# A two-block transformer on one core: the order of work at five seams between stages

## The reference, cut to what matters

```python
mod = cs @ ada_w[l] + ada_b[l]
sh1, sc1, g1, sh2, sc2, g2 = jnp.split(mod, 6, axis=-1)
h = rms_norm(x, norm_mix_g[l]) * (1.0 + sc1[:, None]) + sh1[:, None]
x = x + g1[:, None] * hybrid_mixer(h, w_in[l], w_out[l], ...)
h = rms_norm(x, norm_ffn_g[l]) * (1.0 + sc2[:, None]) + sh2[:, None]
f = swiglu(h, ...) if l % 2 == 0 else moe_ffn(h, ...)
x = x + g2[:, None] * f
...
x = rms_norm(x, final_norm_g)                       # end of the first model
x = x + 0.5 * swiglu_2(rmsnorm(x, ffn1_norm[l]), ffn1_w_gu[l], ffn1_w_down[l])
```

## Time and profile before

| | |
|---|---|
| median of 3 runs | 2380.55 us (2379.64 to 2385.55) |
| profiled execution | 2394.42 us, of which span 2393.1 us, mean granted TensorE clock 0.974 |
| TensorE matmul | busy 2298.8 us, 96% of the span, 10628 instructions |
| VectorE | busy 1705.5 us, 71% |
| ScalarE | busy 1416.7 us, 59% |
| DMA | 571.55 MB, mean 239 GB/s |

### The profile page before, as it was taken

How to read it: one execution, slowest core, us unless ns; L and a number is a source line. 1 busy time by engine, 2 the same in 40 slices (tenths; PEclk the granted TensorE clock), 3 DMA queues, 4 the chain that set the end, 5 groups by cost and what they waited for, 6 DMA issues and landing times.

```text
span 2393.1 us, 34697 instructions
## 1 busy us (share of the span) xinstructions
PE 2298.8 (96%) x10628; PEld 1884.6 (79%) x10628; DVE 1705.5 (71%) x2223; ACT 1416.7 (59%) x2071; POOL 42.2 (2%) x69
## 2 busy tenths in 40 slices
PE   6998999998999999999999989999999999889999
PEld 5776887777888888888887778877888888767887
DVE  4776877766889999998999955577555555744554
ACT  4645444555787777778777754465544544565443
POOL 1000111000000000000000000000000000000000
PEclk8999999999999999999999999999999999979999
DMA  8855887754999999999999945553565555412651
GB/s 300 278 174 181 282 301 267 249 158 109 347 360 356 352 366 353 358 358 354 367 349 357 349 152 185 191 167 117 183 193 177 184 184 176 151 50 62 211 191 55
DMA packets 411218, 571.55 MB, mean 239 GB/s; under 512 B 28111, under 2 KB 324481, under 8 KB 410978
## 3 DMA queue, kind: packets, MB, share of 16 engines
q1 hardware_dynamic: 401200, 543.13, 67.9%
q0 software_dynamic: 6960, 23.79, 3.3%
q10 hardware_dynamic: 2946, 3.22, 0.4%
HBM read 568.99 MB, written 1.05 MB: 238 GB/s over the span
## 4 chain that ended last, share of the span: by engine, by line
PE 85%; DVE 7%; ACT 5%; issue 2%; SPq 1%; DMA 0%; ACTq 0%; DVEq 0%
PE bank L348 76%; DVE lo L327 2%; ACT hi L325 1%; PE bank L543 1%; PE bank L2660 1%; ACT xn L102 1%; SPq L274 1%; PE bank L810 1%; PE bank L2787 1%; ACT aT_hi L102 1%; PE bank L1857 0%; PE bank L2729 0%; DMA raw<-ada_w 0%; DVE small L102 0%; PE bank L1819 0%
## 5 line engine op out<-in xcount | busy, mean ns | idle before, releaser
L327 DVE TENSOR_TENSOR lo<-raw,hi 128x1024 fp32r<-128x1024 f32 x997 | 1177.6, 1221 | 192.1 <-ACT hi L325 178.1
L325 ACT ACTIVATE hi<-raw 128x1024 fp32r<-128x1024 f32 x997 | 1004.4, 1054 | 108.4 <-PE bank L348 99.3
L348 PE MATMUL bank<-hi,aT_hi 128*128 128x512 f32 (+1 forms) x2016 | 814.8, 404 | 23.7 <-DVE aT_lo L102 10.6
L348 PE MATMUL bank<-hi,aT_lo 128*128 128x512 f32 (+1 forms) x2016 | 791.7, 393 | 0.0
L348 PE MATMUL bank<-lo,aT_hi 128*128 128x512 f32 (+1 forms) x2016 | 790.9, 392 | 0.0
L348 PEld LDWEIGHTS bank<-hi,aT_hi 128*128 128x128 f32 x2016 | 383.9, 190 | 106.9 <-issue 17.6
L348 PEld LDWEIGHTS bank<-hi,aT_lo 128*128 128x128 f32 x2016 | 383.1, 190 | 81.8
L348 PEld LDWEIGHTS bank<-lo,aT_hi 128*128 128x128 f32 x2016 | 384.6, 191 | 74.6 <-issue 1.7
L348 PE MATMUL bank<-hi,hidT_hi 128*128 128x512 f32 x792 | 310.1, 392 | 0.9 <-DVE hidT_lo L2668 0.9
L348 PE MATMUL bank<-hi,hidT_lo 128*128 128x512 f32 x792 | 308.4, 389 | 0.0
L348 PE MATMUL bank<-lo,hidT_hi 128*128 128x512 f32 x792 | 308.3, 389 | 0.0
(11 more groups left out here) (330 smaller groups left out, 1609.3 us busy)
## 6 DMA issues: line engine op xcount, KB each, us to landing
raw<-moe_w_gate SPq DMA_DIRECT2D x352, 256.0 KB
raw<-moe_w_up SPq DMA_DIRECT2D x352, 256.0 KB
raw<-moe_w_down SPq DMA_DIRECT2D x176, 512.0 KB
raw<-ffn_w_gu SPq DMA_DIRECT2D x352, 256.0 KB
raw<-ffn_w_down SPq DMA_DIRECT2D x110, 512.0 KB
raw<-ada_w SPq DMA_DIRECT2D x56, 512.0 KB
raw<-w_in SPq DMA_DIRECT2D x56, 512.0 KB
ada_slot<-ada_w POOLq DMA_DIRECT2D x40, 512.0 KB, 6.4
```

The lines of the kernel that those rows point to most:

```text
L325: act.activation(hi[u % SPL][:, :], raw[r % RAW][:, :], ACTF.Copy).then_inc(hi_done, 1)
L327: dve.tensor_tensor(lo[u % SPL][:, :], raw[r % RAW][:, :], hi[u % SPL][:, :].bitcast(F32), ALU.subtract).then_inc(lo_done, 1)
L348: ins = pe.matmul(bank, left[a], right[b], start=first and n == 0, stop=last and n == 2)
```

## The change

It moves work at five seams.

1. `FFN_SLABS` has (0, 11) ahead of (1, 9), so slab (0, 11) ends one step sooner. `at_end` keeps the look-ahead alone. `second_bias` and `second_conditioning` move into the last two steps; there the row of (0, 11) is copied by ScalarE to `mod_rows` and both gate halves are added in one instruction. Of slab (1, 9) the second half, its column sums, four columns of `mod_cols` and the second gain are done by `last_ada_columns` in slot 5 of layer 1's mixer, on bank 5.
2. `modulated_first` calls `run_late(1)` and `run_late()` sooner, between the subtractions.
3. The second tile's squares are summed in one instruction of 1024 (`rstd_whole`), not two halves.
4. In `route_tokens` the second tile's low part (`split_lo(1)`) stands behind the one-hot matrices and the count, and the weights stand in front of the pair. `first_pair` starts with six products that need no second low part; TensorE loads the count between the second and the third bank.
5. In `normed_final` the squares of the first tile's `x` are summed ahead of the second tile's copies, the other three sums behind them.

```diff
-FFN_SLABS = [(0, 10)] + [(1, n) for n in (0, 1, 2, 3, 6, 7, 8, 9)] + [(0, 11)]
+FFN_SLABS = [(0, 10)] + [(1, n) for n in (0, 1, 2, 3, 6, 7, 8)] + [(0, 11), (1, 9)]
...
         def at_end():
-            begin(STEPS - 1, 0, 1)
-            end(STEPS - 1)
             look_ahead(UNITS_D)
...
         h = hi_pair(0, 2, a)
+        run_late(1)
+        done += lo_pair(0, 2, h)
         split_to(st["use"] + 3)
         a = full_pair(0, full_act, 0, turned[2], 4, gain, bias, marks)
-        done += lo_pair(0, 2, h)
         h = hi_pair(0, 4, a)
-        run_late(1)
+        done += lo_pair(0, 4, h)
+        run_late()
         split_to(st["use"] + 4)
-        run_late()
...
+    def rstd_whole(t):
+
+        ss, v, r = tiny(1), tiny(1), tiny(1)
+        a = ACT.run([x_mark[t]], act.activation, xn[:, t, :], x[:, t, :], ACTF.Square, accum_out=ss)
+        a = ACT.run([a], act.activation, v, ss, ACTF.Sqrt, bias=eps_col[:, :], scale=1.0 / D)
+        return r, DVE.run([a], dve.reciprocal, r, v)
...
+    def last_ada_columns():
+
+        n = STEPS - 2
+        ada_sums(n, 0, 1)
+        PE.need(*bank_mark[5])
+        pe.wait_ge(ada_steps, 8 * n + 8)
+        for j in range(4):
+            ins = pe.matmul(psum[5][:, j:j + 1], ada_sum[n % 2][:, j * P:(j + 1) * P], ones_sq[:, 0:1], start=True, stop=True)
+        m = PE.did(ins)
+        m = DVE.run([m], dve.tensor_tensor, mod_cols[:, 28:32], psum[5][:, 0:4], bias_cols[:, 28:32], ALU.add)
+        bank_mark[5] = (m,)
+        mod_marks[:] = [modulated_gain(1, 1, range(8), m)]
...
+            if n == 5 and layer:
+                last_ada_columns()
...
             one_hots()
             busy = count_most(full)
             e, ready = ratio()
-            PE.need(busy)
-            pe.reg_load(most[mybir.EngineType.PE], busiest_i[0:1, 0:1])
-            first_pair()
+            first_hi[:] = [parts[1]]
+            split_lo(1)
+            route["weights"] = weights(eq4, w4, out, e, ready)
+            first_pair(lambda: (PE.need(busy), pe.reg_load(most[mybir.EngineType.PE], busiest_i[0:1, 0:1])))
             split_to(st["use"] + 6)
-            route["weights"] = weights(eq4, w4, out, e, ready)
...
         run_late()
+        sq = square(0, x, pp, [x_mark[0], (moe_y, 4)])
         split_to(st["use"] + 4)
...
-            gained(0)
+            g0 = gained(0)
             done = plain_tile(1, groups, gain)
-            a = gained(1)
+            g1 = gained(1)
+            a = square(0, xg, ss, [g0, sq])
+            b = square(1, x, pp, [x_mark[1]])
+            a = square(1, xg, ss, [g1, b])
```

More of the change, by code:

```diff
@@ L1039, in ada_out @@
         acc = ada_sum[n % 2]
-        if n in (0, STEPS - 2):
+        if n in (0, STEPS - 3):
             pe.matmul(psum[3][:, :], ones_sq[:, :], acc[:, :], start=True, stop=True).then_inc(ada_added, 1)
+            part = slice(0, SLAB) if n == 0 else slice(SLAB, D)
+            dst, src = mod_rows[:, part], psum[3][:, :]
         else:
@@ L1182, in accs_ripe, with second_bias, second_conditioning @@
         return max(0, (st["acc"] - 2) // 4)
[L1184 to L1199, removed]
+    def second_bias():
+        PE.need(bias_in[0])
+        pe.wait_ge(ada_rows, STEPS - 4)
+        pe.transpose(psum[3][:, 32:64], bias_pieces[:, :], ident[0:32, 0:32])
+        ada_out(STEPS - 4)
+        bias_mark[:] = [ACT.run([], act.activation, bias_cols[:, :], psum[3][:, 32:64], ACTF.Copy)]
+    def second_conditioning():
+        dve.wait_ge(ada_rows, STEPS - 2)
+        m = DVE.run(bias_mark, dve.tensor_tensor, mod_cols[:, 0:28], ada_cols[:, 0:28], bias_cols[:, 0:28], ALU.add)
+        DVE.need(gates_in[0])
+        gates_mark[:] = [DVE.did(dve.tensor_tensor(gates[:, 1, :], gates[:, 1, :], mod_rows[:, 0:D], ALU.add))]
+        bank_mark[3] = (m,)
+        mod_marks[:] = [modulated_gain(1, 0, range(8), m)]
     def store_tile(t):
@@ L2259, in route_tokens @@
         r, r_mark, xT_marks, logits, parts = {}, {}, {}, {}, {}
+        first_hi = []
         top, idx = tiny(NT * 8), tiny(NT * 8)
@@ L2353, in one_hots, with first_pair @@
                     route["hot"] = one_hot(DVE, z, t, 2 * z + t)
-        def first_pair():
+        def first_pair(load_count):
             hot = route["hot"]
@@ L2360, in first_pair, with term @@
             mark = {}
[L2361 to L2367, removed]
+            banks = (6, 7, 4, 5)
+            def term(i, kk, n):
+                k, (t, part) = 2 * i + kk, ((0, 0), (0, 1), (1, 0), (1, 1))[n]
+                return pe.matmul(psum[banks[i]][:, kk * S:(kk + 1) * S], xn_split[part][:, t, k * P:(k + 1) * P],
+                                 onehot[:, t, :, :].rearrange("p z s -> p (z s)"), start=n == 0, stop=n == 3)
+            PE.need(hot, parts[0], *first_hi)
+            for i in range(2):
+                PE.need(*bank_mark[banks[i]])
+                for n in range(3):
+                    term(i, 0, n)
+            PE.need(parts[1])
+            for i in range(4):
+                PE.need(*bank_mark[banks[i]])
+                for kk, n in [(0, 3)] if i < 2 else [(0, n) for n in range(4)]:
+                    term(i, kk, n)
+                for n in range(4):
+                    ins = term(i, 1, n)
                 mark[i] = PE.did(ins)
+                if i == 1:
+                    load_count()
             out, hi_mark, lo_mark = {}, {}, {}
@@ L2896, in end @@
         def end(n, i=0):
-            if n == STEPS - 1:
-                second_conditioning(n)
+            if n == STEPS - 3:
+                second_bias()
+            elif n == STEPS - 2:
+                PE.need(*bias_mark)
+                ada_out(n - 1)
+                second_conditioning()
             elif n > 0:
```

19 lines of the change are left out of this document (8 added, 11 removed).

## The result

| | before | changed |
|---|---|---|
| median, 20 runs each | 2386.45 us (2377.74 to 2391.41) | 2379.41 us (2373.73 to 2387.49) |
| ratio | | 0.9977, 95% interval 0.9967 to 0.9988 |
| profiled execution | 2394.42 us, span 2393.1 | 2380.89 us, span 2379.6 |
| mean granted clock, profiled | 0.974 | 0.980 |

The change made the kernel faster by 5.5 us as the ratio has it (2.9 to 7.9), 7.0 us between the medians. 6.1 us was forecast and lies inside; the likeliest verdict given, no change, does not hold, since the interval excludes 1.

What follows compares the result with a forecast made beforehand. TensorE was taken to bound the kernel, with 85% of the chain of waits, so seams count by what it loses there. 1.3 + 4.2 - 9.1 + 2.0 + 7.7 = 6.1 us off 2380.55 gave 2374.4 us, range 2367.5 to 2380.5.

Steps and rivals of the forecast that it cites:

- Term 3: Slot 5 of the mixer: TensorE waits for VectorE's four sums, then columns and slow matmuls follow; cost 9.1 us.
- Rival A: Slot 5 of the mixer: VectorE is not behind, TensorE waits about 2 us; time 2368.2 us; chance 0.12.
- rival C: Mixer slots 8 to 11: VectorE's debt comes back to TensorE, slower than before, 2381.9 us; chance 0.08.
- Terms 1 and 2: Layer 0's feed-forward part: additions come sooner, gaining 1.3 us at its start and 4.2 us at its end.
- Term 4: Routing: VectorE reaches the branch sooner and its wait there stays 4.34 us; gain 2.0 us, bounds 1.0 and 2.5.
- Term 5: Behind the experts: `r_keep` 4.65 us sooner, TensorE's 4.07 us gap becomes 1.2, clock stays up; gain 7.7 us.
- Rival B: Behind `normed_final`: the clock falls there too, so the gain is 4.65 us; time 2377.5 us; chance 0.15.

Runs made afterwards that it cites:

- early_sums: The changed kernel with the second half of the last slab summed right behind the mixer's first slab, not in slot 5; 2371.9 us, ratio 0.9945.
- p1_slabs: The kernel before with only the slab order, second conditioning in the last steps and last slab's columns in slot 5; 2393.78 us, ratio 1.0031.
- p4_routing: The kernel before with only the second low part behind the one-hot matrices and the weights ahead of the pair; 2382.77 us, ratio 0.9984.
- p5_final: The kernel before with only the sums of squares in `normed_final` moved behind the copies; 2378.78 us, ratio 0.9969.
- weights_last: The changed kernel with the seven instructions of the weights back right ahead of the branch; 2380.06 us, ratio 0.9966.
- p23_start: The kernel before with only the second tile's additions between the subtractions and its squares summed in one instruction; 2383.53 us, ratio 0.9975.

## Why the prediction was right or wrong

- **Term 3 (9.1 us at slot 5)** was right: wait 5.55 us for 5.56, columns 1.84 for 1.84, the stretch 9.6 us longer. early_sums shows the cause: the sums' place in VectorE's queue. Rival A falls (TensorE waited 5.55 us, not 2), and C too: from 445 to 531 us the changed kernel's TensorE has no gap of 0.9 us or more.
- **Terms 1 and 2 (1.3 and 4.2)** were right: 8.65 to 7.33 us for the first, a gap of 3.07 us for the forecast 3.1 in the second. Between the two turns p1_slabs takes 197.36 us, p4_routing 201.40 and p5_final 201.38: 4.0 us for term 2. The other 1.1 of the -5.19 are fewer matmuls at the lower level behind the first turn (3 or 4 in place of 8), and p4_routing and p5_final have them too, with no change there.
- **Term 4 (2.0)** was too small: 3.46 us. The failed step is "I take the gap as what VectorE needs to load its register and branch", as a constant of 4.34 us. It became 3.06 with two long low parts right in front of the branch. The end of VectorE's work ahead of the branch came 2.18 us sooner, as forecast (2.05), but not by the forecast's halves of 1.05 and 1.0: in weights_last, where only the low part has moved, it already came 2.03 us sooner, and moving the weights too gave 0.15. That sum was right by luck.
- **Term 5 (7.7)** was too large. `r_keep` came 4.7 us sooner (forecast 4.65), the gap was 1.51 us for 1.2, so TensorE went on 4.4 us sooner. The failed step is "a gap of 1.2 us is of the size that left the clock at 1.00, so the 3.05 us come too": the clock fell behind the short gap in five of the six profiles that have it unfilled, for about half as long, so only 1.3 us came in the changed kernel's. Rival B was half right.
- **The sum**: 1.3 + 4.0 - 9.6 + 3.5 + 5.7 = 4.9 us by the changed kernel's trace, 5.8 at equal clock, 5.5 by the ratio, 6.1 forecast. The two wrong sizes cancel (1.5 too little, 2.0 too much), and that is luck. The profiled executions lie 13.5 us apart; the other 8.5 us are no gain of a seam: 0.3 us ahead of the feed-forward part, 1.1 of clock behind its second turn, 2.6 of clock behind the first expert's wait, and 4.5 in the last stretch.
- **The numbers** failed at "A measurement of this kernel can tell about 0.3%": with 20 runs a side it tells 0.11%, and a gain of 0.23% is no longer "the same". The level, a median of three, was 5.9 us off: the runs' granted clock moves the kernel by more than the change does. And the range, 2367.5 to 2380.5, is said to hold most of rival C, whose own time, 2381.9, lies outside it.

## What to carry to other kernels

Put the work of a side chain so early into its engine's queue that its consumer comes well behind it: the same four sums cost 8.7 us in slot 5 and nothing 7 us earlier, counted from the mixer's first turn. Ahead of a branch, try a long instruction last, with the small chained ones further up; in all profiles here the wait was shorter so. Filling a wait to keep the clock up can pay only where no other engine's chain sets the next wait. And compare runs of about the same granted clock before you believe a difference of a few us.

## What the runs showed of the hardware that I had not expected

- Behind gaps of about the same length the clock falls in one execution and not in another. Ahead of the first expert it fell behind 2.40 us (p4_routing) and not behind 3.56 (p23_start); behind `normed_final` a 1.50 us gap left it up in early_sums alone.
- The mean granted clock of an execution lies between 0.974 and 0.985 for one kernel; the medians of its slowest and fastest group above lie 10.6 us apart.
- VectorE's wait behind one branch is 1.74 to 4.87 us in versions of the same program, by what stands in front of it, while 1.8 to 2.1 us lie between an instruction packet's start and its restart each time. ScalarE's longest idle time around the same branch of the changed kernel is 1.12 us. It ends 1.84 us behind another such packet, which starts while the second of ScalarE's two high parts ahead is still running.
